# Dilated and sparse attention of a decoder layer in native f32, two heads at once on two halves of the array

## What is computed

```python
h = rmsnorm(x, norm_mix); proj = h @ w_in                    # 1024 -> 5656 columns
# sparse part: 8 heads of 64 in 2 groups; every query head has three branches
y_a = g0 * attn(q, k_cmp, v_cmp) + g1 * attn(q, k_slc, v_slc) + g2 * attn(q, k_win, v_win)
# dilated part: 3 groups (dilation 1, 4, 16) x 4 heads of 64, window of 128 steps
for g in range(3):
    o[g], lse[g] = banded_softmax_attention(q[g], k[g], v[g], dilation=(1, 4, 16)[g])
y_b = sum(o[g] * softmax(lse)[g] for g in range(3))
merged = sigmoid(gm_a) * (y_a @ w_up_nsa) + sigmoid(gm_b) * (y_b @ w_up_dil)
x = x + merged @ w_out
x = x + (silu(h2 @ w_gate) * (h2 @ w_up)) @ w_ffn_out        # h2 = rmsnorm(x), d_ff 2816
return rmsnorm(x, norm_final)
```

## Time and profile before

| | us |
|---|---|
| median of 3 runs | 851.26 (851.17 to 853.23) |
| profiled execution, its own time | 850.63 |
| span in the profile, first to last instruction | 848.3 |
| PE busy | 812.0 (96%) |
| DVE busy | 449.1 (53%) |
| ACT busy | 298.7 (35%) |

### The profile page before, as it was taken

How to read it: one execution, slowest core, us unless ns; L and a number is a source line. 1 busy time by engine, 2 the same in 40 slices (tenths; PEclk the granted TensorE clock), 3 DMA queues, 4 the chain that set the end, 5 groups by cost and what they waited for, 6 DMA issues and landing times.

```text
span 848.3 us, 10708 instructions
## 1 busy us (share of the span) xinstructions
PE 812.0 (96%) x4087; PEld 679.8 (80%) x4087; DVE 449.1 (53%) x867; ACT 298.7 (35%) x531; POOL 37.5 (4%) x52
## 2 busy tenths in 40 slices
PE   5999999999999789999999899999999999999993
PEld 4878899789878678888888688888888888888883
DVE  4646332654888899875734644444444444433336
ACT  6111154243356666563223522222222222222213
POOL 2301100000000010001210000000000000000003
PEclk9999999999999999999999999999999999999998
DMA  7931336320311011116343133333333332222202
GB/s 240 315 100 50 100 66 158 90 92 2 101 50 50 1 51 51 38 38 198 118 131 100 49 100 97 91 90 91 91 90 95 98 99 100 100 99 99 99 0 99
DMA packets 98500, 79.03 MB, mean 93 GB/s; under 512 B 16880, under 2 KB 92704, under 8 KB 98464
## 3 DMA queue, kind: packets, MB, share of 16 engines
q1 hardware_dynamic: 98368, 78.52, 30.9%
q10 hardware_dynamic: 96, 0.02, 0.0%
HBM read 75.34 MB, written 3.19 MB: 93 GB/s over the span
## 4 chain that ended last, share of the span: by engine, by line
PE 85%; DVE 6%; ACT 4%; DMA 2%; issue 1%; SPq 0%; ACTq 0%; DVEq 0%
PE bank L1302 25%; PE bank L1303 25%; PE bank L1304 25%; ACT probs L640 2%; PE bank L1402 2%; PE bank L1519 1%; PE bank L1498 1%; PE bank L1451 1%; PE bank L1483 1%; DVE probs L1122 1%; ACT probs_t_hi L720 1%; DMA xs<-in_x_dram 1%; PE bank L1366 1%; PE bank L1322 1%; DVE k_stack L1090 0%
## 5 line engine op out<-in xcount | busy, mean ns | idle before, releaser
L1302 PE MATMUL bank<-h_hi,w_hi 128*128 128x512 f32 x352 | 138.1, 392 | 3.0 <-DVE h_lo L874 3.0
L1304 PE MATMUL bank<-h_hi,w_lo 128*128 128x512 f32 x352 | 137.7, 391 | 0.0
L1303 PE MATMUL bank<-h_lo,w_hi 128*128 128x512 f32 x352 | 137.5, 391 | 0.0
L1302 PE MATMUL bank<-n_hi,w_hi 128*128 128x512 f32 x288 | 114.9, 399 | 1.3 <-DVE gm L938 1.3
L1304 PE MATMUL bank<-n_hi,w_lo 128*128 128x512 f32 x288 | 112.3, 390 | 0.0
L1303 PE MATMUL bank<-n_lo,w_hi 128*128 128x512 f32 x288 | 112.3, 390 | 0.0
L819 DVE TENSOR_TENSOR w_lo<-w_raw,w_hi 128x2048 fp32r<-128x2048 f32 (+2 forms) x30 | 67.2, 2240 | 62.2 <-ACT w_hi L578 61.8
L1302 PEld LDWEIGHTS bank<-h_hi,w_hi 128*128 128x128 f32 x352 | 66.5, 189 | 17.4 <-issue 3.5
L578 ACT CAST w_hi<-w_raw 128x2048 fp32r<-128x2048 f32 (+2 forms) x30 | 55.6, 1854 | 67.6 <-PE bank L1304 56.0
L766 ACT ACTIVATE tanh_g<-gate_scaled 128x512 f32<-128x512 f32 x22 | 13.9, 632 | 185.9 <-DVE gate_scaled L1245 185.9
L1303 PEld LDWEIGHTS bank<-h_lo,w_hi 128*128 128x128 f32 x352 | 66.5, 189 | 14.1 <-issue 0.2
(11 more groups left out here) (207 smaller groups left out, 1264.1 us busy)
## 6 DMA issues: line engine op xcount, KB each, us to landing
w_raw<-in_w_ffn_in_dram SPq DMA_DIRECT2D x44, 512.0 KB, 4.6
w_raw<-in_w_in_dram SPq DMA_DIRECT2D x39, 512.0 KB, 4.8
w_raw<-in_w_ffn_out_dram SPq DMA_DIRECT2D x22, 512.0 KB, 3.6
w_raw<-in_w_out_dram SPq DMA_DIRECT2D x8, 512.0 KB, 4.1
xs<-in_x_dram SPq DMA_DIRECT2D x4, 512.0 KB, 6.3
wck_k<-in_w_ck_dram SPq DMA_DIRECT2D x1, 2048.0 KB, 10.6
wck_v<-in_w_cv_dram SPq DMA_DIRECT2D x1, 2048.0 KB, 17.4
w_raw<-in_w_in_dram SPq DMA_DIRECT2D x8, 256.0 KB, 4.2
```

Of the source, the lines that this page charges most:

```text
L1302: pe.matmul(dst, w[0], x_[0], start=start, stop=False)
L1303: pe.matmul(dst, w[0], x_[1], start=False, stop=False)
L1304: return pe.matmul(dst, w[1], x_[0], start=False, stop=stop)
```

## The change

Heads are now treated in pairs. The sparse stage has 20 steps of exactly 512 score columns per head, five for each pair `j`, `j + 4` (the two groups' heads, rows 0 to 63 and 64 to 127 of `qa` and `ka`); the tables `NSA_STEPS` and `DIL_STEPS` name which query tiles a step has. The scores of the two heads go to banks 0 and 1, in turns, in native f32 from unsplit queries and keys. Transposes are 4 per head into banks 4 and 5, ACT copies each once, and the outputs go in turns to rows 0 to 63 and 64 to 127 of one bank (6, or 3 for odd pairs), in native f32. The splits of queries, keys, values, probabilities and compressed probabilities are gone. The dilated stage has 8 steps of both heads instead of 12 of one, built in the same way. Fillers in the sparse stage are cut into halves of 12 matmuls (`part`), alternate between banks 2 and 7, and are evacuated by a job of their own (`evac`).

```diff
-Q_OFF = [0, 128, 384, 768]
-S_PLACE = [(1, 384), (2, 0), (1, 0), (0, 0)]
-K_OFF = [0, 512, 1024, 896]
-K_PLACE = [(3, 0), (4, 0), (5, 0), (4, 384)]
-T_CUTS = [(0, 512), (512, 1024), (1024, 1280)]
+NSA_STEPS = [((0, 3),), ((0, 0), (0, 2)), ((0, 1), (1, 1)), ((1, 3),), ((1, 0), (1, 2))]
+NSA_N = 4 * len(NSA_STEPS)
 
 B_OFF = [0, 128, 384, 640]
-B_PLACE = [(1, 256), (0, 0), (0, 256), (1, 0)]
-
-
-
-BESIDE_DIL_SCORES = (2, 2, 2, 2, 2, 3)
+
+DIL_STEPS = [(0, (1, 2)), (0, (3, 0)), (1, (0, 1, 2, 3)), (2, (0, 1, 2, 3))]
+
+
+
+BESIDE_DIL_SCORES = (3, 3, 3, 4)
 BESIDE_MERGE = 2
-SPLIT_AT = 11
-BESIDE_DIL_OUT = (0, 0, 1, 1, 1, 0)
-BESIDE_CMP = (3, 1, 0, 0, 2, 0, 0, 0, 0, 0, 1)
-BESIDE_NSA = (1, 1, 1, 0, 0, 0, 1, 1, 0, 1, 1, 0, 1, 1, 1, 0)
+BESIDE_DIL_OUT = (0, 1, 1, 1)
+BESIDE_CMP = (3, 1, 0, 0, 2, 0, 0, 0, 1)
+HALVES_NSA = (2, 2) + (1,) * 18
+HALVES_END = (2, 2)
...
+    halves = [(n, 4 * h) for n in tile for h in range(2)]
+    ended = []
+
+    def parts(count):
+        for _ in range(count):
+            n, k = halves.pop(0)
+            jobs.append(("part", (n, k)))
+            if k:
+                ended.append(n)
+
+    def drain():
+        jobs.extend(("evac", n) for n in ended)
+        ended.clear()
+
+    for n in range(NSA_N):
         jobs.append(("scores", n))
+        drain()
         if n > 1:
             jobs.append(("out", n - 2))
         if n:
             jobs.append(("turn", n - 1))
-
-        if n % 2 == 0 and n < 2 * NH - 2:
-            jobs.append(("split_q", n // 2 + 1))
-        if n in (6, 7):
-            jobs.append(("split_k", n - 4))
-        if n in (0, 1, 8, 9):
-            jobs.append(("split_v", n if n < 2 else n - 6))
-        beside(BESIDE_NSA[n])
-    beside(1)
-    jobs += [("out", 14), ("turn", 15)]
-    beside(1)
-    jobs.append(("out", 15))
-    beside(1)
-    assert next(tile, None) is None
+        parts(HALVES_NSA[n])
+    jobs += [("out", NSA_N - 2), ("turn", NSA_N - 1)]
+    drain()
+    parts(HALVES_END[0])
+    jobs.append(("out", NSA_N - 1))
+    drain()
+    parts(HALVES_END[1])
+    drain()
+    assert not halves
     return jobs
...
+        TILE_BANK[_n[0]] = 7 if _n[0] % 2 else 2
...
+        def nsa_segments(n):
+
+            c, found = 0, []
+            for b, i in NSA_STEPS[n % 5]:
+                found.append((b, i, c, P * (i + 1)))
+                c += P * (i + 1)
+            return found
...
+                segments = nsa_segments(n)
+                for r in range(2):
+                    act.wait_ge(s_max, 2 * n + r + 1)
+                    for k, (b, i, c, w) in enumerate(segments):
+                        v = len(segments) * r + k
+                        q = sp[n % 2][:, r, c:c + w]
+                        ins = act.activation(q, q, ACT.Exp, scale=-1.0, bias=ust[:, n % 2, 0, v:v + 1],
+                                             accum_out=ust[:, n % 2, 1, v:v + 1])
+                ins.then_inc(s_exp, 1)
...
                 elif job == "turn":
-                    if n:
-                        act.wait_ge(o_ready, n)
-                    else:
-                        act.wait_ge(do_ready, 12)
-                    for k, (a, b) in enumerate(T_CUTS):
-                        act.wait_ge(t_ready, 3 * n + k + 1)
-                        act.copy(pthi[:, a:b], ps[3 + k][:, 0:b - a]).then_inc(t_hi, 1)
-                    if n < 15:
-                        nsa_exps(n + 1)
-                    else:
+                    if n == 0:
+                        act.wait_ge(do_ready, 8)
+                    elif n > 1:
+                        act.wait_ge(o_ready, n - 1)
+                    for r in range(2):
+                        act.wait_ge(t_ready, 2 * n + r + 1)
+                        act.copy(npt[:, n % 2, r, :], ps[4 + r][:]).then_inc(t_evac, 1)
...
             def scores(n):
-                dve.wait_ge(s_ready, n + 1)
                 if n == 0:
-                    dve.wait_ge(dt_ready, 24)
+                    dve.wait_ge(dt_ready, 16)
                 if n >= 2:
-                    dve.wait_ge(t_ready, 3 * (n - 1))
-                for i in range(TT):
-                    bank, c = S_PLACE[i]
-                    w = P * (i + 1)
-                    ins = dve.tensor_tensor_reduce(
-                        sp[n % 2][:, Q_OFF[i]:Q_OFF[i] + w], ps[bank][:, c:c + w], nbias[:, n // 2 % 2, 384 - P * i:512],
-                        -1.0, -NEG, ALU.add, ALU.min, ust[:, n % 2, 0, i:i + 1])
-                ins.then_inc(s_max, 1)
+                    dve.wait_ge(t_ready, 2 * n - 2)
+                segments = nsa_segments(n)
+                for r in range(2):
+                    dve.wait_ge(s_ready, 2 * n + r + 1)
+                    for k, (b, i, c, w) in enumerate(segments):
+                        v = len(segments) * r + k
+                        ins = dve.tensor_tensor_reduce(
+                            sp[n % 2][:, r, c:c + w], ps[r][:, c:c + w], nbias[n // 5 % 2][:, r, 384 - P * i:512],
+                            -1.0, -NEG, ALU.add, ALU.min, ust[:, n % 2, 0, v:v + 1])
+                    ins.then_inc(s_max, 1)
...
+                for r in range(2):
+                    for k, (b, i, c, w) in enumerate(segments):
+                        v = m * r + k
+                        q = sp[n % 2][:, r, c:c + w]
+                        ins = dve.tensor_scalar(q, q, ust[:, n % 2, 3, v:v + 1], None, ALU.mult)
+                    ins.then_inc(p_ready, 1)
+
+            def pair_out(j):
+
+                dve.wait_ge(o_ready, 5 * j + 5)
+                dve.tensor_copy(ya[:, j, :], ps[3 if j % 2 else 6][:]).then_inc(y_evac, 1)
...
             def dil_scores(n):
-                m = n % 6
-                g, hh, t = m // 2, m % 2, n // 6
+                g, tiles = DIL_STEPS[n % 4]
+                t = n // 4
                 tile_evacuated(LAST_TILE[U_KB + g])
                 if n:
-                    pe.wait_ge(ds_max, n)
-                rows = slice(HD * hh, HD * hh + HD)
-                q, k = qb[rows, 2 * g + t, :], kb[rows, 2 * g + t, :]
-                for i in range(TT):
+                    pe.wait_ge(ds_max, 2 * n)
+                c = 0
+                for i in tiles:
                     lo = P * (i - 1) if g == 0 and i else P * i
-                    bank, c = B_PLACE[i] if g == 0 else (0, P * i)
-                    ins = pe.matmul(ps[bank][:, c:c + P * (i + 1) - lo], q[:, P * i:P * i + P], k[:, lo:P * (i + 1)],
-                                    start=True, stop=True)
-                ins.then_inc(ds_ready, 1)
+                    w = P * (i + 1) - lo
+                    for hh in range(2):
+                        rows = slice(HD * hh, HD * hh + HD)
+                        ins = pe.matmul(ps[hh][:, c:c + w], qb[rows, 2 * g + t, P * i:P * i + P],
+                                        kb[rows, 2 * g + t, lo:lo + w], start=True, stop=True)
+                        if i == tiles[-1]:
+                            ins.then_inc(ds_ready, 1)
+                    c += w
...
             def scores(n):
-                h, b = n // 2, n % 2
                 if n == 0:
-                    pe.wait_ge(pc_lo_ready, 2)
+                    pe.wait_ge(pct_ready, 2)
                 else:
-                    pe.wait_ge(s_max, n)
-                pe.wait_ge(q_lo, h + 1)
-                pe.wait_ge(k_lo, 2 * (h // 4) + b + 1)
-                for i in range(TT):
-                    bank, c = S_PLACE[i]
-                    w = P * (i + 1)
-                    for k in range(2):
-                        ins = pe.matmul(ps[bank][:, c:c + w], qst[h % 2][:, P * i:P * i + P], kst[:, b, k, 0:w],
-                                        start=(k == 0), stop=(k == 1))
-                ins.then_inc(s_ready, 1)
+                    pe.wait_ge(s_max, 2 * n)
+                segments = nsa_segments(n)
+                for b, i, c, w in segments:
+                    for r in range(2):
+                        ins = pe.matmul(ps[r][:, c:c + w], qa[rows_of(r), n // 5, P * i:P * i + P],
+                                        ka[rows_of(r), b, 0:w], start=True, stop=True)
+                        if (b, i) == segments[-1][0:2]:
+                            ins.then_inc(s_ready, 1)
 
             def turn(n):
-                pe.wait_ge(p_ready, n + 1)
                 if n:
-                    pe.wait_ge(t_lo, 3 * n)
+                    pe.wait_ge(t_evac, 2 * n)
                 else:
-                    pe.wait_ge(do_evac, 12)
-                for js in ((0,), (1, 3), (2,)):
-                    for j in js:
-                        bank, c = K_PLACE[j]
-                        for i in range(j, TT):
-                            a = Q_OFF[i] + P * j
-                            ins = pe.transpose(ps[bank][:, c + P * (i - j):c + P * (i - j) + P],
-                                               sp[n % 2][:, a:a + P], ident[:])
+                    pe.wait_ge(do_evac, 4)
+                for r in range(2):
```

(35 more changed lines are left out.)

434 lines of the change are left out of this document (184 added, 250 removed).

## The result

| | us |
|---|---|
| the changed kernel, median of 4 runs | 830.17 (828.53 to 832.10) |
| the kernel before, beside it | 851.21 (850.60 to 853.23) |
| ratio, with its 95% interval | 0.975 [0.9721, 0.9778] |
| profiled execution, its own time / span | 828.53 / 826.7 |

What follows compares the result with a forecast made beforehand. PE was taken as the bound, busy 812.0 of 848.3 us, with some 10 us of waits for DVE. Terms -15.2 + 4.8 - 2.0 + 4.5 = -7.9 took 850.63 to 842.7, 843 for the median; range 833 to 854.

Steps and rivals of the forecast that it cites:

- Row halves run together: Scores of two heads on rows 0 to 63 and 64 to 127: full overlap assumed; dilated scores save 7.4 us.
- second rival: Scores blocks: row halves overlap only in part, a pair taking 1.13 us; 848 or 849 for the kernel; chance 0.12.
- The slower rival: Every scores block: row halves don't overlap, the second head waits for the first; +15, 858 us; chance 0.10.
- Column pairs: Outputs of two heads in column halves: a pair costs what one costs, 0.11 us per record; dilated outputs save 7.2.
- open loads: Rival, outputs: weight loads can't run beside their half's matmul, 0.055 us per pair, +12, 851 us; chance 0.03.
- Dilated stage, -15.2 of PE work and +4.5 of waits: Dilated scores, outputs and transposes save 7.4, 7.2 and 0.6 us of PE work; waits become 6.0 against 1.5.
- The three terms named for new waits: Dilated stage: three value-filler waits of 0.8 us each, 1.8 at transposes near the end, 0.6 more after the first merge.
- Sparse PE work, +4.8: Sparse stage: 16 steps of 3.60 us, 57.6, become 20 steps of 3.12, 62.4 us.
- Sparse waits: Sparse stage: PE's waits, taken as all for DVE, fall from 10.0 to 8 us, -2.0; ends 1 and 18.
- DVE's round: Sparse stage: DVE needs 31.3 us for five steps against PE's 30.2, so PE waits 1.1 in each of 3.6 groups.
- Waits vanish: Rival: PE may run half a step ahead, leaving waits of 2 us in sparse, 5 in dilated; 836 us; chance 0.15.
- wrong: its waits under 3 us in all: Sign against the forecast: PE's waits in the sparse stage come to under 3 us in all.

## Why the prediction was wrong in its size

1. *Row halves run together: right,* and it carried the forecast. In the step above the records of the two heads start 0.007 us apart (259.224 and 259.231, 265.091 and 265.098), and a step's 512 columns for both heads (four records) take 1.06 us with their changeover, where 0.87 + 0.20 was laid out. The partial overlap of the second rival, and with it the estimate from the Trainium skill's factor, did not appear. The slower rival (no overlap, 858) fell too.
2. *Column pairs: right.* Sixteen records in 1.03 us, one load each, leave no room for open loads. The rule of the Trainium skill ("TensorE: Matmul & The Clock Gate", Part 3, "What overlaps and what doesn't"), by which column halves could not hide their loads, disagrees with this row; the measurement decides.
3. *Dilated stage, -15.2 of PE work and +4.5 of waits: -10.7; measured -12.0.* The waits came to 2.7 us (the first two windows above), not 6.0. The value fillers, where I had put three waits of 0.8, waited 0.3. Against that, 3.4 us of the stage ran at half clock, which cost 1.7; kernels built on the changed one, with the same dilated stage and no such stretch in it, took 128.7 to 129.3 us. So that -10.7 came within 1.3 us is in part luck. (The three terms named for new waits, 2.4 + 1.8 + 0.6, also add up to 4.8 and not to 4.5.)
4. *Sparse PE work, +4.8: right;* the floor rose from 132.2 to 136.8 and the period is the one laid out.
5. *Sparse waits, "8 us against 10.0: -2.0": wrong.* It was 0.9 against 14.1, -13.2. This step alone is the miss of 11 us. Four things failed in it.
   - The waits of before were read as span less busy time, which left out 4 us.
   - They were all put down to unscaled probabilities, which are 4.1 of 10.0. The others were for the subtraction, the reductions and the fillers' bank.
   - DVE's round was laid out by durations end to end: "5.7 us", "4.0 by the same rows". Records of DVE and ACT overlap their successors. In the step above the four reductions take 1.39 us from 260.50 (not 2.0), ACT's exponentials 2.0 from 261.31 (not 2.76; the prediction has 2.84 for equal segments), and the whole from the first reduction to the end of the scalings 4.5. A step of one segment takes 3.6 by the same trace. With the prediction's own 5.3 for weight splits and 0.9 for the pair, five steps are 3 x 4.5 + 2 x 3.6 + 6.2 = 26.9 us, an estimate, against PE's 30.2 (which the trace confirms: from one pair's compressed products to the next are 30.3 us). DVE has slack where the prediction said that its round "is slightly the longer". The run with 2.9 us more on DVE agrees. By the prediction's durations 1.85 us of the addition fit into DVE's wait for ACT in a step of two segments and 1.07 in a step of one; the rest makes 31.3 + 3 x 1.02 + 2 x 1.80 = 38.0 us against 30.2, nearly 30 us of waits in the stage. The stage grew by 10.6.
   - The prediction costed the halves of the fillers at about 1 us, as a matter of banks, and named ACT's new order only as a burden ("outputs held by a late copy on ACT"). Undone, they bring back 9.0, 5.1 and together 28.1 us. The largest piece of the change stood in the diff, and what it takes away had no term in the sum.
6. *"Waits vanish", 836, was the rival that came true,* in its mechanism and not in its size: it too was built on 10.0 us and left 2 us in the sparse stage and 5 in the dilated one. It had 0.15 of the chances and lies 6 us above the measured time.
7. *"After the sparse stage nothing changes":* its work is the same; in the two profiled executions the feed-forward part differs by 1.6 us, by the clock, as told below.

The line "wrong: its waits under 3 us in all" was met. A step's PE work was 3.1 us, as laid out.

## What to carry to other kernels

When two engines hand work back and forth, lay out the loop by distances between starts, and ask which operation of the next step stands in a queue behind one that needs the step before. Here moving the exponentials ahead of the copies broke such a loop, and evenly spread filler covered the latency that this order left. In the changed kernel either alone took 19 to 23 of 28 us, and only both took nearly all; in the kernel before, halves alone took 3 of 14, and the order made it slower. So try such edits one by one and together, on both sides of a change. The simpler arithmetic (one copy, two buffers) with the pairs was worth 0.3 us in the stage and the order that goes with it 5.1. A change whose PE work grows in a stage can still shorten it, if what it drops is what PE waited for.

## What was not expected of the hardware

**Half clock after an idle stretch.** In the kernel before PE stands for some 3 us at 470 and then runs at half clock from 474.8. In after the same idle time is there and the clock stays full, but a stretch at half clock stands behind the wait of 2.0 us that ends at 161.6. Windows of before, then of after:

```profile
470.00:474.80 4.80, 1.76 (x10) 1.33 (x11) 4.23 (x16) 4.71 (x16) 0.00 (x0) 1.00 0.00 0
474.80:478.30 3.50, 3.50 (x10) 2.76 (x9) 1.34 (x9) 3.41 (x5) 0.00 (x0) 0.51 0.00 0
```

```profile
161.74:165.15 3.41, 3.41 (x23) 2.75 (x23) 3.06 (x17) 2.44 (x9) 0.00 (x0) 0.50 0.93 255
```

Each costs 1.6 to 1.8 us. The kernel with both edits undone had 17 us of such stretches in its sparse stage, the old kernel with the order of the change 30.6. The run with four additions had none between 24 us and its last matmul, though it kept the wait of 2.0 us and that of 3.0 at the start of the feed-forward part. So an idle stretch of some 2 us on PE can cost nearly as much again.

It is not a property of the kernel alone. From the first up-projection to the end of the last matmul all kernels here do the same work. Profiled executions without such a stretch in this part took 443.7 us for it, those with 3.4 us of it 445.1 to 445.9, those with 6.8 us of it 446.3 to 446.6. And single executions of the kernel before, beside the runs, range from 849.26 us at a mean granted clock of 0.994 to 858.98 at 0.983. A difference of 2 us between two profiled executions can be this and nothing else. Which idle stretch is followed by half clock stays open.

**Halves of the array overlap without being in turns.** In the run with outputs apart, matmuls of the second column half start beside the last ones of the first (at 262.80, where the first half's last record starts at 263.12). What sets how early they start, no run here shows.
